# A fused transformer kernel: router products with 128 columns, a second expert's biases ahead of the ranks, latent projections as three reduced products, and a gate product with its weight rests last

## The reference

```
proj = rmsnorm(x, g_mix) @ w_in                       # 1024 x 3616
q_a, k_a, v_a, c_q, c_kv, k_pe, gate_a, gate_b = split(proj)
y_a = moba_attention(rope(rmsnorm(q_a)), rope(rmsnorm(k_a)), v_a)
q_b = rmsnorm(c_q, g)  @ w_uq                         # latent 256 -> 768
kv  = rmsnorm(c_kv, g) @ w_ukv                        # latent 128 -> 1024
y_b = causal_attention(q_b, k_b, v_b)
x = x + (sigmoid(gate_a)*(y_a @ w_a) + sigmoid(gate_b)*(y_b @ w_b)) @ w_out

h = rmsnorm(x, g_ffn)
logits = h @ w_router + b_router                      # 1024 -> 32
top 4 of 32 experts per token; for each expert e and its tokens:
    gu = h @ w_gate_up[e] + b_gate_up[e];  y = swiglu(gu) @ w_down[e] + b_down[e]
x = x + weighted sum

x = x + sigmoid(rmsnorm(x, g_ple) @ w_ple_gate) * (p @ w_ple_proj)
```

## Time and profile before

| | |
|---|---|
| median of 3 runs | 1750.84 us (1750.6 to 1751.12) |
| the profiled execution, its time | 1750.17 us |
| its span in the trace | 1748.4 us |
| PE busy | 1649.3 us (94%) |
| DVE busy | 704.5 us (40%) |
| ACT busy | 574.6 us (33%) |
| POOL busy | 24.2 us (1%) |
| moved from memory | 544.00 MB |
| mean granted clock of TensorE | 0.994 of full |

### The profile page before, as it was taken

How to read it: one execution, slowest core, us unless ns; L and a number is a source line. 1 busy time by engine, 2 the same in 40 slices (tenths; PEclk the granted TensorE clock), 3 DMA queues, 4 the chain that set the end, 5 groups by cost and what they waited for, 6 DMA issues and landing times.

```text
span 1748.4 us, 20393 instructions
## 1 busy us (share of the span) xinstructions
PE 1649.3 (94%) x8902; PEld 1037.5 (59%) x8903; DVE 704.5 (40%) x879; ACT 574.6 (33%) x794; POOL 24.2 (1%) x37
## 2 busy tenths in 40 slices
PE   9999999898889999998888898999999999999998
PEld 7788533333344544533232333388888998988887
DVE  5897411121212112111020211177664865567663
ACT  7576200111111111100000111185554765455552
POOL 0000000000000000000000000010000000000000
PEclk9999999999999999999999999999999999999999
DMA  7559999999999999999999999955555424445552
GB/s 250 173 182 298 386 417 428 426 428 427 427 426 428 427 425 429 426 427 429 427 428 427 428 417 425 412 176 185 193 193 178 159 97 137 163 136 180 192 192 97
DMA packets 119643, 546.41 MB, mean 313 GB/s; under 512 B 5808, under 2 KB 64304, under 8 KB 93984
## 3 DMA queue, kind: packets, MB, share of 16 engines
q1 hardware_dynamic: 118224, 540.96, 77.9%
q0 software_dynamic: 1040, 4.00, 0.7%
q10 hardware_dynamic: 288, 0.11, 0.0%
HBM read 544.00 MB, written 1.05 MB: 312 GB/s over the span
## 4 chain that ended last, share of the span: by engine, by line
PE 47%; DMA 29%; ACT 2%; DVE 1%; issue 1%; DVEq 0%; ACTq 0%; SPq 0%
DMA ring<-in_w_down 29%; PE PS L1057 8%; PE PS L653 8%; PE PS L1242 6%; PE PS L660 4%; PE PS L1001 3%; PE PS L638 1%; PE PS L639 1%; PE PS L640 1%; PE PS L605 1%; PE PS L607 1%; PE PS L606 1%; PE PS L1285 1%; PE PS L677 1%; PE PS L1257 1%; PE PS L1480 1%
## 5 line engine op out<-in xcount | busy, mean ns | idle before, releaser
L1001 PE MATMUL PS<-ring,work 128*64 128x512 f32 x1984 | 439.9, 595 | 27.9 <-DMA ring<-in_w_gate_up 27.9
L2105 DVE TENSOR_TENSOR ring<-ring,ring 128x2048 fp32r<-128x2048 f32 (+2 forms) x129 | 286.9, 2233 | 223.1 <-ACT ring L1495 222.9
L1001 PEld LDWEIGHTS PS<-ring,work 128*64 128x64 f32 x1984 | 137.6, 137 | 309.8 <-issue 248.1
L1495 ACT CAST ring<-ring 128x2048 fp32r<-128x2048 f32 (+2 forms) x130 | 241.2, 1866 | 177.5 <-DMA ring<-in_mem_w_kv 87.3
L1057 PE MATMUL PS<-ring,work 128*64 128x512 f32 x992 | 229.0, 604 | 49.7 <-DMA ring<-in_w_down 36.5
L1057 PEld LDWEIGHTS PS<-ring,work 128*64 128x64 f32 x992 | 72.1, 138 | 192.0 <-issue 162.0
L2542 DVE TENSOR_SCALAR work<-PS 128x512 f32<-128x512 f32 x32 | 22.1, 690 | 348.4 <-PE PS L1001 348.4
L1766 ACT ACTIVATE work<-work 128x512 f32<-128x512 f32 x32 | 20.1, 630 | 368.0 <-DVE work L2542 368.0
L2438 DVE TENSOR_TENSOR work<-PS,work 128x512 fp32r<-128x512 f32 x32 | 22.1, 692 | 241.9 <-ACT work L1703 241.9
L1242 PE MATMUL PS<-ring,work 128*128 128x512 f32 x432 | 98.2, 389 | 0.0
L1242 PEld LDWEIGHTS PS<-ring,work 128*128 128x128 f32 x432 | 81.1, 188 | 16.8
(11 more groups left out here) (464 smaller groups left out, 2343.8 us busy)
## 6 DMA issues: line engine op xcount, KB each, us to landing
ring<-in_w_gate_up SPq DMA_DIRECT2D x124, 2048.0 KB, 20.6
ring<-in_w_down SPq DMA_DIRECT2D x61, 2048.0 KB, 21.2
ring<-in_ffn_w_gu SPq DMA_DIRECT2D x44, 1024.0 KB, 5.1
ring<-in_w_in SPq DMA_DIRECT2D x27, 1024.0 KB, 5.2
ring<-in_ffn_w_down SPq DMA_DIRECT2D x22, 1024.0 KB, 4.8
ring<-in_w_out SPq DMA_DIRECT2D x8, 1024.0 KB, 5.2
ring<-in_mem_w_kv SPq DMA_DIRECT2D x8, 1024.0 KB, 16.9
work<-in_w_gate_up SPq DMA_DIRECT2D x3, 2048.0 KB, 14.6
```

The source lines that it names most:

```text
L1001: t = e.matmul(PS[hf * 64:hf * 64 + 64, bank, :], XG[g % 2][:, 2 * kp + kk, i * 64:(i + 1) * 64], raw_chunk(w, kk)[:, c0 + hf * 512:c0 + h ...
L1495: e.copy(hi(j), raw(j)).then_inc(*act.now(("hi", j)))
L2105: e.tensor_tensor(lo(j), raw(j), hi(j).bitcast(F32), ALU.subtract).then_inc(*dve.now(("lo", j)))
```

## The change

Five edits, in the order in which they run:

1. **Latent projections.** `uq` and `ukv` are split now: ACT copies both (1,536 and 1,024 elements in each partition) right after `v`, and POOL makes both rests. The latents are split too: DVE makes `latT[0]` and, in three more instructions, `latT[1]` (`latT_rest`). `small` makes three fp32r products in place of each float32 one, with those of the latents' rests last. The first half of `uq` goes to the banks of `c`, so that it waits for `act["c", 1]`, and the wait for `act["gate", 0, 1]` comes ahead of the second half. `hi_to(14)` on ACT and `lo_to(13)` on DVE move behind the copies of the transposed q and k.
2. **Router logits.** Each product takes the columns of four chunks, 128 in place of 32. The address of the output is moved by 32 columns with each chunk so that the wanted 32 always fall on columns 96 to 127; the others are not read.
3. **Biases.** `biases(1)` runs directly behind `biases(0)`, ahead of the wait for the mask. Its banks were those of the third and fourth gather, which now use the banks of the first and second again. The idle products around the ranks are 3 and 3 in place of 2 and 2.
4. **End of the experts.** `combine_last` has 6 idle products in place of 10.
5. **The gate.** `first_gate` makes all 48 products of both parts: for each part first hi times hi, then the activations' rests, then the weights' rests. The hi times hi products wait for ACT's chunks one by one. ACT makes the hi of the second part behind all four turned pairs.

```diff
-        add("uq", [("w_uq", 0, 2, 0, 768)], split=False)
-        add("ukv", [("w_ukv", 0, 1, 0, 1024)], split=False)
+        add("uq", [("w_uq", 0, 2, 0, 768)])
+        add("ukv", [("w_ukv", 0, 1, 0, 1024)])
...
-        return i != self.of["ple_gate", 0][0]
+        return i not in [self.of[k][0] for k in (("ple_gate", 0), "uq", "ukv")]
...
-        first_gathers = (BM, BDN, 0, 3)
+        first_gathers = (BM, BDN, BM, BDN)
...
+            def small(c0, nk, i, n0, n, h, o, key, last):
...
+                for k in range(nk):
+                    for w in (whi, wlo):
+                        e.matmul(o, latT[0][:, c0 + k, hs], w[:, k, ns], start=k == 0 and w is whi, stop=False,
+                                 skip_group_check=True)
+                for k in range(nk):
+                    e.wait_ge(*dve["latT_rest", c0 + k])
+                    t = e.matmul(o, latT[1][:, c0 + k, hs], whi[:, k, ns], start=False, stop=k == nk - 1, skip_group_check=True)
...
-                    t = e.matmul(PS[:, LGT, h * 32:(h + 1) * 32], hT32[:, k, h * 128:(h + 1) * 128], wr[:, k, :],
-                                 start=k + h == 0, stop=k == 7, skip_group_check=True)
+                    k0 = min(k, 4)
+                    o = h * 256 + LG0 - 32 * (k - k0)
+                    t = e.matmul(PS[:, LGT, o:o + 128], hT32[:, k, h * 128:(h + 1) * 128],
+                                 wr[:, k0:k0 + 4, :].rearrange("p k n -> p (k n)"), start=k + h == 0, stop=k == 7,
+                                 skip_group_check=True)
...
             biases(0)
-            idle_products(0, 2)
+            biases(1)
+            idle_products(BM, 3)
             e.wait_ge(*dve["mask"])
...
-                idle_products(BU, 10)
+                idle_products(BU, 6)
...
+                for part, i in enumerate(of["ple_gate", 0]):
+                    whi, wlo = chunks(hi(i), i), chunks(lo(i), i)
+                    e.wait_ge(*act["hi", i])
+                    for z in range(2):
+                        for kk in range(4):
...
+                            if z == 0:
+                                e.wait_ge(*act["pleT", k // 2, k % 2])
...
-            hi_to(14)
+            hi_to(13)
...
+            hi_to(14)
...
-            lo_to(13)
             for i in (0, 2):
                 e.wait_ge(*pe["qk_t", i])
                 e.tensor_copy(qkTa[:, 2 * i:2 * i + 2, :],
                               PS[:, i, :].rearrange("p (c t) -> p c t", c=2)).then_inc(*dve.now(("qkT", i)))
+            lo_to(13)
...
             e.dma_start(cst[:, 128:C_HM], d["cst"][:, 128:C_HM]).then_inc(tables_in, 16)
+            lo_to(of["ukv"][0])
             e.wait_ge(tables_in, 16)
```

More of the change, by code:

```diff
@@ L410, in build @@
         PO = 14144
-        lat, latT = W(PO, 2, 384), W(PO + 768, 3, 256)
+        lat, latT = W(PO, 2, 384), (R32(PO + 768, 3, 256), R32(PO + 1536, 3, 256))
         QB, KB, KV = 17216, 18752, 20288
@@ L803, in tensor @@
             turn_pair(lat, 2, 1, 5, ("lat_t", 1))
-            e.wait_ge(*act["gate", 0, 1])
-            e.wait_ge(*dve["latT", 0])
+            e.wait_ge(*act["c", 1])
             (uq,), (ukv,) = of["uq"], of["ukv"]
@@ L1179, in first_gate @@
             def first_gate():
[L1181 to L1186, removed]
-                    for h in range(2):
[L1188 to L1196, removed]
+                for part, i in enumerate(of["ple_gate", 0]):
+                    whi, wlo = chunks(hi(i), i), chunks(lo(i), i)
+                    e.wait_ge(*act["hi", i])
+                    for z in range(2):
+                        for kk in range(4):
+                            k = 4 * part + kk
+                            if z == 0:
+                                e.wait_ge(*act["pleT", k // 2, k % 2])
+                            elif kk % 2 == 0:
+                                e.wait_ge(*dve["pleT", k // 2])
+                            for h in range(2):
+                                e.matmul(PS[:, h, :], xT[z][:, k, h * 128:(h + 1) * 128], whi[:, kk, :], start=k + z == 0,
+                                         stop=False, skip_group_check=True)
+                    e.wait_ge(*ready(i))
+                    for h in range(2):
+                        for kk in range(4):
+                            t = e.matmul(PS[:, h, :], xT[0][:, 4 * part + kk, h * 128:(h + 1) * 128], wlo[:, kk, :],
+                                         start=False, stop=part == 1 and kk == 3, skip_group_check=True)
+                        if part or h:
+                            t.then_inc(*pe.now(*([("ple", 0, h)] if part else []), *([("w", i)] if h else [])))
             pe.stage("ple")
@@ L1208, in tensor @@
             first_gate()
-            for h in range(2):
-                tok_part(xT, of["ple_gate", 0], 1, h, PS[:, h, :], ("ple", 0, h),
-                         [dve["pleT", 2 + i] for i in range(2)] if h == 0 else ())
             def ple_last(part, h):
@@ L2252, in vector @@
                 e.wait_ge(*pe["lat_t", i])
-                e.tensor_tensor(latT[:, 2 * i:2 * i + m, :], PS[:, 4 + i, 0:m * 256].rearrange("p (c t) -> p c t", c=m),
+                e.tensor_tensor(latT[0][:, 2 * i:2 * i + m, :], PS[:, 4 + i, 0:m * 256].rearrange("p (c t) -> p c t", c=m),
                                 bc(gain("mla_q_lat_norm", 2 * i, m), [128, m, 256], 2), ALU.mult).then_inc(*dve.now(("latT", i)))
+                e.wait_ge(*dve.last)
+                for c in range(2 * i, 2 * i + m):
+                    o = (c % 2) * 256
+                    e.scalar_tensor_tensor(out=latT[1][:, c, :], in0=PS[:, 4 + i, o:o + 256], scalar=gain("mla_q_lat_norm", c),
+                                           in1=latT[0][:, c, :].bitcast(F32), op0=ALU.mult,
+                                           op1=ALU.subtract).then_inc(*dve.now(("latT_rest", c)))
             for b in range(2):
@@ L2258, in vector @@
                     e.tensor_copy(qb2[:, h, b * 384:(b + 1) * 384],
-                                  PS[:, (6, 7, 0, 1)[2 * b + h], 0:384]).then_inc(*dve.now(("uq", 2 * b + h)))
-            lo_to(13)
+                                  PS[:, 6 * b + h, 0:384]).then_inc(*dve.now(("uq", 2 * b + h)))
             for i in (0, 2):
```

29 lines of the change are left out of this document (12 added, 17 removed).

## The result

The changed kernel takes 1756.58 us (median of 9 runs, 1754.81 to 1757.65) against 1750.6 (9 runs, 1749.08 to 1752.14): a ratio of 1.0035, 95% interval 1.0026 to 1.0043. It is slower, clear of the noise, and lies above the predicted range (1746.6 to 1753.3). The profiled execution took 1757.64 us with a span of 1755.8, 7.4 more than the span before.

A forecast was written before the change was run, and what follows sets the result against it. PE was taken to bound the kernel up to 160 us and behind 1134 us, memory transfers the experts between; +1.3 (attention), -1.5 (router) and -0.75 (end) sum to -0.95, giving 1749.9 us, range 1746.6 to 1753.3.

The forecast's parts named there:

- Rests on POOL: POOL's two weight rests beside DVE's rope: `latT` 1.0 us late, ends 0 and 2.6.
- POOL holds DVE up: Rival, chance 0.12: POOL excludes DVE at the rope, `latT` 4.0 us late, stage costs 4.3; 1752.9 us.
- Three products: Latent projections on PE: 24 products of 384 columns and 12 of 512 take 6.9 us, saving 1.8.
- The rest of part 13 moved: DVE behind the copies of q and k: L2266 starts 0.3 us later, PE's 1.9 us given back.
- The gain given back at part 15: PE waits at 92.90 for DVE's rest of part 15, giving back its 1.9 us in full.
- the attention stage keeps its gain: Rival, chance 0.12: DVE's chain does not set PE's wait at 92.90, so 1.9 us stay; 1746.7 us.
- Router: Wider logits keep the clock full and the second expert's biases move into the mask's wait: -1.5 us (-1.7 to +1.1).
- the clock falls all the same: Rival, chance 0.14: at the router the clock still halves, +1.05 in place of -1.5; 1752.4 us.
- the router edits change nothing: Rival, chance 0.12: experts are memory bound and the hole at 212 has another cause; 1751.4 us.
- End: End of experts and gate: six idle products let PE start 0.75 us earlier, regrouping gains nothing; -0.75 us (-1.2 to 0).

The follow-up runs named there:

- pool_late: The changed kernel with POOL's rests begun only when the rope on DVE is done; 1754.23 us.
- dve_rests: The changed kernel with the rests of the query and key-value weights on DVE behind the rope, none of them on POOL; 1751.09 us.
- dve_ahead: dve_rests with `lo_to(13)` ahead of the copies of the transposed q again, and 40 small matmuls ahead of the crowded check's branch; 1747.88 us.
- ahead15: dve_ahead with the rest of part 15 on DVE ahead of the division of the probabilities instead of behind it; 1747.16 us.
- latent_only: The kernel before with the latent projections' edit alone, router and gate as before; 1757.96 us.
- before_moved17: The kernel before with 17 matmuls of 16 columns ahead of the crowded check's branch, adding 34 recorded PE instructions; 1751.80 us.
- wide_logits: The kernel before with the router's logits over four chunks' columns alone; 1749.52 us.

## Why the prediction was wrong

- **The step that failed** is *Rests on POOL*: "I take the middle, 1.0 us late, and keep 0 and 2.6". `latT` was 3.45 us late. I scaled one row, L2392 beside POOL's casts, as a slowdown, and called the middle of two bounds an estimate. It is no slowdown but exclusion: the rope lost 4.42 + 3.40 - 1.23 - 1.22 = 5.4 us, close to POOL's 3.50 + 2.3. That was the rival "POOL holds DVE up", at 0.12, and its sign, rope instructions much beyond 2 us, came. The page cited there, "VectorE: DVE Perf Modes" of the Trainium skill, was right about the shared interface; the Trainium skill's page "SBUF — State Buffer", section "SBUF: two separate sides", says that whichever starts first keeps the pair for the whole instruction. The rows agree: 3.50 and 4.68 us in `pool_late`. Read so, the price was the 5.7 us that the rival had added up from the earlier trace rows. What I held against that rival, POOL's rest at 1136, proves nothing: the DVE instructions beside it (L2568, L2111) read PSUM and at most one tile in SBUF.
- **What the rival left out** is the clock. It forecast 4.3 us for the stage, and 7.2 came. With the wait of 4.26 us the first half of the projections ran at half clock: 9.31 us in place of 7.0. The 2.27 us ahead of 99.05 brought a second fall; from there to the logits it took 87.8 us where it had been 86.8. The stage adds up: 0.3 for the moved rest, 3.5 for PE's late start (68.27 against 64.79), 2.4 for the projections (9.31 against 6.9) and 1.1 behind 99.05 make 7.3.
- **Three products**: forecast 6.9 us, measured 7.03 at the full clock. Right.
- **The rest of part 13 moved**: forecast 0.3 us, with PE's whole gain given back. In `dve_rests`, where POOL makes no rests here and DVE idles 2.00 us ahead of the copies of q and k, so that the other moved rests do not count, L2282 is 12.8 us behind the latents' transposes (12.4 before): 0.45. The wait of 2.31 that forms at 93.83 was foreseen, the fall of the clock behind it (0.50 from 96 to 98 us) not: 1.4 us at the logits. The term was right as a shift and too small as a price.
- **The gain given back at part 15**: right, and shown by `dve_ahead` and `ahead15`; the rival "the attention stage keeps its gain" fell.
- **Router**: -1.5 forecast, -1.6 measured; clock at 1.00, hole at 212 gone. The first expert's products start 9.8 us behind the first logits in place of 11.0, and these 1.2 us and the 0.45 counted for the second biases make the 1.6. Right. The rivals "the clock falls all the same" and "the router edits change nothing" fell.
- **End**: -0.75 forecast, -0.8 measured, all of it from the idle products. Right.
- **Not in the sum at all**: 1.4 to 1.9 us between medians for where PE's code lies at the branch. No edit there, so I had not opened those rows; the program's length ahead of the branch was an effect of the change that the order showed.

What stays open: why the experts' stretch varies by some 2.3 us between executions of kernels that are alike there. The profiled execution of `ahead15` lies 2.2 us above its median, and that lies in the same stretch (954.8 us from the logits to the last idle products, 952.3 in `dve_ahead`). How the branch and the block are handled inside is inferred from where the wait falls, not seen.

## What to carry to other kernels

Before moving a two-input instruction to POOL, add its whole duration to DVE's two-input instructions that run beside it, in place of scaling them by a factor, and ask what a late DVE does to PE. Price each new PE wait of some microseconds twice: its length, and the half clock behind it; where the wait can't go, idle products returned about 2 us here, of some 7. Where a kernel branches, look at the first products behind the branch after every edit ahead of it, however far away.

## What the runs showed of the hardware

- DVE and POOL exclude each other by whole instructions when both read two tiles in SBUF: 1.22 us became 4.42 and 3.40, and POOL's 3.50 became 6.24. The one that waits may wait for more than one instruction: POOL's 6.24 us hold L2162 and L2163, which took 1.22 each. Even a POOL cast of 32 elements took 1.21 us while DVE ran the rope's last instruction, and 0.20 in `pool_late`, with no such instruction on DVE.
- Behind the branch of the crowded check PE goes on only after a packet of the instruction queue. In windows of 0.1 us the packets show at 346.6 and 352.2 in the changed kernel, and PE resumed at 349.26 and 354.82. In the five kernels with a second wait (the changed one, `latent_only`, `dve_rests`, `pool_late`, `before_moved17`) they are 5.6 to 6.1 us apart, and PE resumed 2.4 to 2.8 us behind each. The kernel before has them at 341.0 and 346.6 and stops only for the first. The window from 352 to 354 us of the changed kernel:

```profile
q8 instruction: 1, 0.02, 3.3%
```

  The Trainium skill's page "Runtime: NRT & Kernel Launch", section "Instruction fetch mechanics", says that code comes in blocks of 256 instructions and that a taken branch to a place not yet held breaks the fetching ahead. The waits fit this; no run here shows the size of a block. The runs add that the block after the one branched to is not ahead either: with the boundary 2 or 4 multiplies behind the branch's biases PE waited 2.8 to 3.2 us; with it 19 multiplies on by count, in the kernel before, or ahead of the branch's end, not at all.
- The clock can fall with PE fully busy on products of 32 columns (0.56 with PE busy 0.50 of 0.50 us) and stay at 1.00 when those products have 128 columns and PE then waits (busy 2.12 of 3 us in `wide_logits`).
